# Gate projections as three-term products in four of five attention kinds

## The reference, cut to what matters

```
gates  = sigmoid(u @ w_in[:, C_GATE:])        # first block: three gates of 1024 features
merged = gates0 * y_mla + gates1 * y_hg + gates2 * y_mem
...
merged = sigmoid(ga) * (ya @ w_branch[0]) + sigmoid(gb) * (yb @ w_branch[1]) + sigmoid(gc) * (yc @ w_branch[2])
```

## Time and profile before

| | |
|---|---|
| median of 3 runs | 3121.75 us (3121.09 to 3124.9) |
| profiled execution, its own time | 3122.34 us |
| its span, first to last instruction | 3120.6 us |
| TensorE busy | 2942.3 us (94%), 21202 matmuls |
| VectorE busy | 1689.9 us (54%) |
| ScalarE busy | 1201.8 us (39%) |
| mean granted TensorE clock | 0.970 |
| mean DMA rate | 153 GB/s |

### The profile page before, as it was taken

How to read it: one execution, slowest core, us unless ns; L and a number is a source line. 1 busy time by engine, 2 the same in 40 slices (tenths; PEclk the granted TensorE clock), 3 DMA queues, 4 the chain that set the end, 5 groups by cost and what they waited for, 6 DMA issues and landing times.

```text
span 3120.6 us, 49209 instructions
## 1 busy us (share of the span) xinstructions
PE 2942.3 (94%) x21202; PEld 2753.3 (88%) x21202; DVE 1689.9 (54%) x2846; ACT 1201.8 (39%) x1806; POOL 12.6 (0%) x20
## 2 busy tenths in 40 slices
PE   5999999999998899999899898999999989899997
PEld 5998788999998778899899896789989979678997
DVE  6656632566665843366665434446666543454665
ACT  4445421343544522144343333324444333332443
POOL 0000000000000000000000000000000000000000
PEclk9999999999999999999999998999999989999998
DMA  6553365555554244455464652345555466334552
GB/s 195 185 166 112 102 156 177 167 182 184 189 166 151 73 123 134 155 178 180 149 209 160 179 137 81 96 148 189 176 166 180 158 168 147 95 94 138 188 179 95
DMA packets 493543, 476.48 MB, mean 153 GB/s; under 512 B 63472, under 2 KB 476688, under 8 KB 493200
## 3 DMA queue, kind: packets, MB, share of 16 engines
q1 hardware_dynamic: 489744, 462.85, 47.8%
q0 software_dynamic: 3584, 10.49, 1.5%
HBM read 467.01 MB, written 6.29 MB: 152 GB/s over the span
## 4 chain that ended last, share of the span: by engine, by line
PE 88%; DVE 6%; ACT 3%; DMA 1%; issue 1%; SPq 0%; DVEq 0%; ACTq 0%
PE ps L787 36%; PE ps L858 32%; PE ps L878 15%; PE ps L960 2%; DVE WL L1550 1%; PE ps L935 1%; PE ps L818 1%; DMA RAW<-in_w_in 1%; ACT WH L1245 1%; SPq L648 0%; ACT REGION L1227 0%; DVE U L1532 0%; DVE U L1533 0%; ACT L1233 0%; DVE REGION L1885 0%
## 5 line engine op out<-in xcount | busy, mean ns | idle before, releaser
L1550 DVE TENSOR_TENSOR WL<-RAW,WH 128x2048 fp32r<-128x2048 f32 (+1 forms) x342 | 761.7, 2234 | 497.9 <-ACT WH L1245 496.0
L1245 ACT ACTIVATE WH<-RAW 128x2048 fp32r<-128x2048 f32 (+1 forms) x342 | 633.2, 1858 | 259.5 <-DMA RAW<-in_ffn_wo 123.0
L858 PE MATMUL ps<-UH,WH 128*128 128x256 f32 x2816 | 402.1, 285 | 29.9 <-ACT WH L1245 24.2
L787 PE MATMUL ps<-REGION,RAW 128*128 128x256 f32 (+3 forms) x1904 | 397.9, 370 | 31.3 <-DVE REGION L2043 13.1
L787 PEld LDWEIGHTS ps<-REGION,RAW 128*128 128x128 f32 (+2 forms) x1904 | 340.0, 191 | 89.1 <-DVE REGION L2043 16.2
L858 PE MATMUL ps<-UH,WL 128*128 128x256 f32 x2816 | 395.5, 284 | 9.3 <-DVE WL L1550 9.3
L878 PE MATMUL ps<-HH,WH 128*128 128x256 f32 x1408 | 394.8, 280 | 2.8 <-DVE WL L1550 2.8
L878 PE MATMUL ps<-HH,WL 128*128 128x256 f32 x1408 | 395.2, 281 | 0.0
L858 PEld LDWEIGHTS ps<-UH,WH 128*128 128x128 f32 x2816 | 365.0, 192 | 33.9 <-issue 29.2
L878 PE MATMUL ps<-HL,WH 128*128 128x256 f32 x1408 | 394.4, 280 | 0.0
L858 PE MATMUL ps<-UL,WH 128*128 128x256 f32 x2816 | 393.5, 283 | 0.0
(11 more groups left out here) (212 smaller groups left out, 2903.3 us busy)
## 6 DMA issues: line engine op xcount, KB each, us to landing
RAW<-in_w_ffn_in SPq DMA_DIRECT2D x88, 1024.0 KB, 5.1
RAW<-in_ffn_wi SPq DMA_DIRECT2D x88, 1024.0 KB, 5.1
RAW<-in_w_in SPq DMA_DIRECT2D x86, 1024.0 KB, 5.4
RAW<-in_w_ffn_out SPq DMA_DIRECT2D x32, 1024.0 KB, 5.2
RAW<-in_ffn_wo SPq DMA_DIRECT2D x32, 1024.0 KB, 5.2
RAW<-in_w_out SPq DMA_DIRECT2D x16, 1024.0 KB, 5.3
RAW<-in_w_ffn_out SPq DMA_DIRECT2D x16, 768.0 KB, 4.5
RAW<-in_ffn_wo SPq DMA_DIRECT2D x16, 768.0 KB, 4.5
```

The costliest lines, as they stand in the source:

```text
L787: last = nc.tensor.matmul(o, a, b, start=i == 0, stop=i == len(terms) - 1)
L858: last = nc.tensor.matmul(bank(n, 0, T), a[:, k, side * P:(side + 1) * P], b[:, k, :], start=i == 0 and k == 0, stop=i == 2 and k == DK - 1)
L1245: nc.scalar.activation(part_high(s), raw[pl.place[s]][:, 0:pl.words[s]], ACT.Copy).then_inc(weights_high, 1)
L1550: v_.tensor_tensor(part_low(s), raw[pl.place[s]][:, 0:pl.words[s]], part_high(s).bitcast(FP), ALU.subtract)\
```

## The change

The gate products of the latent, memory, A and C attentions become split products; those of B stay plain. Their slabs are marked as split in the plan. ScalarE and VectorE each get calls of `feed.to` that cut slab 0 ahead of the attention, and one call at the end of each round i of their loops, to slab `min(3, (i * n_f + 2) // 2)`, where `n_f` is the number of gate products of a unit. In the kinds with 8 units that is slab 1 in round 0, slab 2 in round 2 and slab 3 in round 4; in "mem", with `n_f` = 2, it is slab 1, 2 and 3 in rounds 0, 1 and 2. The places of the slabs and the loads are the same.

```diff
--- before.py
+++ after.py
@@ -278,6 +278,7 @@
 
 
 
+GATE_SPLIT = ("mla", "mem", "A", "C")
 ATTN = {"mla": (8, 1, 1, 1), "mem": (4, 1, 1, 1), "A": (8, 2, 1, 1), "B": (8, 6, 3, 3), "C": (8, 2, 1, 1)}
 
 
@@ -321,7 +322,7 @@
         _, _, f, _, n = attention_numbers(pl.total, kind)
         pl.slab_first[name] = len(pl.slab_last)
         for m in range(1, DK, 2):
-            pl.slab(f[m * ATTN[kind][0] // DK] + m % (DK // ATTN[kind][0]), places=places)
+            pl.slab(f[m * ATTN[kind][0] // DK] + m % (DK // ATTN[kind][0]), split=kind in GATE_SPLIT, places=places)
         pl.products(name, n)
 
     for l in range(DEPTH):
@@ -948,9 +949,14 @@
                         for j in range(DK // units):
                             m = (i + 1) * (DK // units) + j
                             sl = slab_first[name] + m // 2
-                            wait_weights(pe, sl)
-                            product(f[i + 1] + j, [(bank(f[i + 1] + j, 0, T),
-                                                    [(slot(sl, DK, 256)[:, k, m % 2 * P:(m % 2 + 1) * P], U[:, k, :]) for k in range(DK)])])
+                            cols = slice(m % 2 * P, (m % 2 + 1) * P)
+                            if kind in GATE_SPLIT:
+                                wait_split(pe, sl)
+                                terms = feature(parts(sl, DK, 256), UP, DK, cols)
+                            else:
+                                wait_weights(pe, sl)
+                                terms = [(slot(sl, DK, 256)[:, k, cols], U[:, k, :]) for k in range(DK)]
+                            product(f[i + 1] + j, [(bank(f[i + 1] + j, 0, T), terms)])
                     if i >= 0:
                         for b in range(n_t):
                             wait_evicted(pe, t[i] + b)
@@ -1297,6 +1303,9 @@
                 units, n_s, n_t, n_b = ATTN[kind]
                 s, t, f, o, _ = attention_numbers(first[name], kind)
                 n_f = DK // units
+                sl = slab_first[name]
+                if kind in GATE_SPLIT:
+                    feed.to(sl)
                 if merged:
                     for m in range(DK):
                         wait_evicted(act, first[merged] + m)
@@ -1327,6 +1336,8 @@
                     if i < units:
                         for j in range(n_f):
                             half_tanh(f[i] + j, GATE[:, i * n_f + j, :], bank(f[i] + j, 0, T))
+                    if kind in GATE_SPLIT:
+                        feed.to(sl + min(3, (i * n_f + 2) // 2))
 
             def tables():
 
@@ -1449,6 +1460,8 @@
                     n = first[L + f"win{i}"]
                     if i + 1 < len(WIN2):
                         feed.to(slab_first[L + f"win{i + 1 + (WIN2[i + 1][0] in ('gate', 'kv'))}"])
+                    else:
+                        feed.to(slab_first[L + "A"])
                     if kind in ("tiles", "pairs"):
                         for c0, dst, func in ((D_CQ, CQ2, ACT.Copy), (D_BQ, BQ, ACT.Copy),
                                               (D_AK, AK, ACT.Copy), (D_AQ, AQ, ACT.Copy)):
@@ -1650,6 +1663,9 @@
                 units, n_s, n_t, n_b = ATTN[kind]
                 s, t, f, o, _ = attention_numbers(first[name], kind)
                 exps = tally.add("exp_done", 0 if kind == "mem" else units)
+                sl, n_f = slab_first[name], DK // units
+                if kind in GATE_SPLIT:
+                    feed.to(sl)
 
                 def scores(i):
                     qt = par = i % 2
@@ -1954,6 +1972,7 @@
                 dve.wait_ge(normed, l * (DK + 6) + 6)
                 dve.wait_ge(mem_in, 16 * (l + 1))
                 v_.tensor_tensor(MEM_SQ, MEM, MEM, ALU.mult).then_inc(squares_ready, 1)
+                feed.to(slab_first[L + "mla"])
                 merge(L + "hg.out", start=True)
                 causal = con("causal", 2 * P)
 
@@ -2044,6 +2064,7 @@
                 merge(L + "A.out", start=True)
                 wait_evicted(dve, first[L + "win9"])
                 attention(L + "B", "B", 64 ** -0.5, pair_window(4))
+                feed.to(slab_first[L + "C"])
                 merge(L + "B.out")
                 attention(L + "C", "C", 64 ** -0.5, pair_window(12), sinks=vec(f"sinks{l}", 8))
                 merge(L + "C.out", end=True)
```

## The result

| | before | after |
|---|---|---|
| median of the runs | 3123.32 us (3121.09 to 3124.95) | 3184.82 us (3162.75 to 3187.89, 4 runs) |
| profiled execution, its own time | 3122.34 us | 3185.07 us |
| its span | 3120.6 us | 3183.3 us |
| mean granted TensorE clock | 0.970 | 0.956 |

Ratio after over before: 1.0192 [1.0165, 1.0218]. The direction was forecast with 0.90, but 3184.8 us lies above the range (3136 to 3172).

The account below looks back on a forecast made before the run. TensorE was taken to bound the kernel (94% busy, 88% of the chain). Idle 63.9 us less 36.5 saved gave +27.4; with 7 for the clock, 3122.3 became 3156.7, median 3156 us, range 3136 to 3172.

Parts of the forecast that it names:

- The queue order: In the four kinds, splits issued behind the tanh or cut late idle TensorE: 31.94 us per layer of each block.
- the 0.74 us of the latent attention's: Extra idle in round 0, where no output product precedes the transposes; taken from the latent attention, added for A and C.
- The saving of the products: Each of 64 gate products falls from 3.45 to 2.88 us, saving 0.57: 36.5 us, 4.56 per attention.
- the cover of slab 0: Outside "mem", slab 0's cut hides behind `hg.out`, `win15` or `B.out` and costs nothing; uncovered, 4.3 us a time.
- The clock: Half clock after new A and "mem" gaps of 2.5 us or more: 4 of 12 at 1.7 us, 7 us.
- The third rival: The clock falls after every long gap, all 12 in A and "mem", adding 20 us: 3169 us; chance 0.18.
- "mem" rival: In the memory attention only slab 0 is exposed, so "mem" saves 2.4 us rather than losing 7.0: 3134 us; chance 0.10.
- the first rival: Splits hide in VectorE's wait for scores, between `outputs(i - 1)` and `scores(i + 2)`; all 36.5 us return: 3085 us; chance 0.06.

Follow-up runs that it names:

- run 4: Changed kernel with its waits kept, but TensorE doing extra unread matmuls in the gaps of all four kinds; 3146.02 us, ratio 1.01 over the kernel before.
- run 3: Changed kernel with cuts issued ahead of the tanh in latent, A and C, and "mem" cut a slab ahead; 3089.72 us, ratio 0.9914 over the kernel before.
- run 1: Changed kernel with cuts moved ahead of ScalarE's tanh and VectorE's `outputs` in latent, A and C only; 3127.39 us, ratio 1.0028 over the kernel before.
- run 2: Changed kernel with only "mem" altered: slabs 0 and 1 cut during `mem.kv`, rounds 0 and 1 cutting slabs 2 and 3; 3137.05 us, ratio 1.0067.
- runs 7: Changed kernel with the memory attention's gate products left plain; 3142.83 us, ratio 1.0078 over the kernel before.
- run 9: Changed kernel, cuts moved earlier, B split too, extra unread matmuls ahead of B's first transposes and `A.out`; 3080.19 us, ratio 0.9866 over the kernel before.
- 10: Changed kernel with cuts moved earlier and B split too, without extra matmuls, measured beside the one with them; 3090.44 us, ratio 0.9892.

## Why the prediction was wrong

- **The queue order: right.** The waits in the four kinds came at the places forecast and nearly in the sizes: 5.7, 11.0, 8.3 and 5.6 us. Only the first gap of each A and C was too long in the forecast, which gave it the 0.74 us of the latent attention's: in the first layer it measured 2.37 us for A, and not 3.57, and 1.53 for C, and not 2.27. With the clock held (run 4) the net cost is 42.6 - 41.3 = +1.3 us for a latent attention, 45.4 - 38.5 = +6.9 for "mem", 44.2 - 39.7 = +4.5 for A and 43.5 - 42.4 = +1.1 for C, forecast +1.3, +7.0, +4.7 and +0.8. Sum +27.5, forecast +27.4. The saving of the products and the cover of slab 0 are in these sums, so neither term is far off; two split products of "mem" are evicted 2.88 us apart in run 3, as forecast.
- **The failing step is "The clock": "I take 4 of the 12, 7 us."** It measured 34 us. Three things in it were too small. First the count: only gaps of 2.5 us and more were let in, 12 of them, but 26 new gaps are 1.5 us or longer. The 14 left out bring nine events, 31 of the 82 us of half clock; at 0.42 that is an estimated 13 us of time. Second the share of gaps that bring half clock: nine of the 12 that were let in, and not four. Third the length of one event: I took 3.41 us of half clock, and six of these nine are 6.8 us long. Together the 12 bring 51 us of half clock, an estimated 21 us of time, where the step had 7. The price for a microsecond of half clock was nearly right, 0.42 measured where the step had 1.7 / 3.41 = 0.5.
- **The third rival** was the right mechanism with the same count, so its 20 us and the top of the range were too low too. That its 20 us are close to the 21 of its 12 gaps is luck: three of them brought nothing, and six brought twice what it took. An upper bound from 12 gaps was no bound. From 26 gaps at 1.7 us each it would have been 44 us, and the range would have held the time. The range's lower end, 3136, was also 2 us above the "mem" rival that it was said to reach.
- **The other rivals fell.** The splits do not hide where this change puts them, but run 1 shows that the place which the first rival named hides them: its mechanism was false of this kernel and true of a kernel two lines away. Its full 36.5 us did not come back even then; 29.5 did in the stages, and the medians are 29 us apart. "mem" was not a slab ahead; run 2, which makes it so, takes 18.8 us off each memory attention.
- **Still open.** What decides which gaps bring half clock, and for how long, no run shows; none varied the length or the place of a single gap. The 5.02 us wait in run 3 is put down to the load by what it waits for and its long landing; no run moved the load. What moves half clock in parts of the program that no edit touches (174 to 201 us outside the stages in runs 7 and the changed kernel, 14 or 38 ahead of the first latent attention in runs 9 and 10) is open too, and it blurs every comparison of whole times by several microseconds.

## What to carry to other kernels

Price a new gap in TensorE's work twice, as idle time and as what follows at half clock, and count the short gaps too, not the longest ones only (five of the ten between 1.53 and 1.76 us brought half clock): here the second price (34 us) was larger than the net cost of the first (27.5). When work is added for an engine with idle time, ask which instruction it stands behind. The same 32 copies and subtractions made the kernel 1.9% slower behind the tanh and 0.9% faster ahead of it and a slab earlier. A change to one stage in a kernel with such gaps shifts the gaps behind it, so read each stage's clock before a difference is put down to the edit.

## What was not expected of the hardware

- **Useless work that pays.** 482 matmuls that nobody reads took 39 us off the time (run 4), and 148 in run 9 took 7 us off the stretches from A to `B.out`. The Trainium skill (TensorE: Matmul & The Clock Gate, What's actually happening) has idling lead back to the low clock, and the stages agree: 0.80 in A without filler, 1.00 with it.
- **The same gap with two prices.** Identical instructions in two layers took 52.45 and 45.58 us. The spread between executions is not shown to be larger for it: the four runs beside the changed kernel put the kernel before at 3121.09 to 3124.95 us, but the 24 beside the experiments at 3109.47 to 3127.41, and the eight runs of the changed kernel lie between 3162.75 and 3187.89.
